# Sliding-window attention of a two-block network: how the softmax is shared between VectorE and ScalarE, and where a weight split stands

## The reference

```python
def one_block(args):
    qi, ki, vi, i = args
    s = jnp.einsum('bqkgd,bskd->bkgqs', qi, ki) + bias
    valid = in_band & ((i > 0) | key_in_own_block)
    s = jnp.where(valid, s, NEG_INF)
    m = jnp.maximum(s.max(-1, keepdims=True), sk)
    p = jnp.exp(s - m)
    p = p / (p.sum(-1, keepdims=True) + jnp.exp(sk - m))
    return jnp.einsum('bkgqs,bskd->bqkgd', p, vi)
```

## Time and profile before

| | |
|---|---|
| runs of the kernel before | 2300.67 us median of 3 (2295.68 to 2301.12) |
| profiled execution, its own time | 2301.37 us |
| its span in the profile | 2299.6 us |
| TensorE busy | 2152.4 us (94% of the span) |
| VectorE busy | 1436.4 us (62%) |
| ScalarE busy | 1020.3 us (44%) |
| GpSimd busy | 132.0 us (6%) |
| moved by transfers | 342.68 MB, 149 GB/s |

### The profile page before, as it was taken

How to read it: one execution, slowest core, us unless ns; L and a number is a source line. 1 busy time by engine, 2 the same in 40 slices (tenths; PEclk the granted TensorE clock), 3 DMA queues, 4 the chain that set the end, 5 groups by cost and what they waited for, 6 DMA issues and landing times.

```text
span 2299.6 us, 37741 instructions
## 1 busy us (share of the span) xinstructions
PE 2152.4 (94%) x16794; PEld 1955.7 (85%) x16794; DVE 1436.4 (62%) x1586; ACT 1020.3 (44%) x1051; POOL 132.0 (6%) x77
## 2 busy tenths in 40 slices
PE   6799999879999999899989999999998988899998
PEld 5778988769998997897778799899888966888996
DVE  8956655566655554866765665465468487657554
ACT  6564543544543443454553344344334437234442
POOL 1000000000001000400010020020022000102000
PEclk9899999999999999999999999999999999899999
DMA  7144555415555655563310466556555532124753
GB/s 192 17 154 146 183 191 174 147 37 165 184 175 179 205 182 175 165 203 113 125 56 2 147 211 192 177 174 201 180 163 186 165 117 103 39 73 148 216 179 119
DMA packets 259274, 342.68 MB, mean 149 GB/s; under 512 B 23111, under 2 KB 169197, under 8 KB 259111
## 3 DMA queue, kind: packets, MB, share of 16 engines
q1 hardware_dynamic: 253968, 329.95, 44.9%
q0 software_dynamic: 2544, 9.08, 1.3%
q10 hardware_dynamic: 2599, 1.23, 0.4%
HBM read 338.14 MB, written 2.10 MB: 148 GB/s over the span
## 4 chain that ended last, share of the span: by engine, by line
PE 78%; DVE 11%; ACT 6%; issue 2%; DMA 2%; POOL 0%; ACTq 0%; DVEq 0%; POOLq 0%
PE acc L1712 20%; PE acc L1713 20%; PE acc L1714 20%; DVE w_lo L1080 4%; PE acc L1728 3%; PE acc L2176 2%; ACT w_hi L638 2%; DMA raw<-in_w_in 1%; PE acc L2171 1%; PE acc L1735 1%; PE trp L1712 1%; PE acc L1777 1%; PE trp L2176 1%; PE trp L1713 1%; PE trp L1714 1%
## 5 line engine op out<-in xcount | busy, mean ns | idle before, releaser
L1080 DVE TENSOR_TENSOR w_lo<-raw,w_hi 128x2048 fp32r<-128x2048 f32 (+1 forms) x316 | 737.0, 2334 | 510.4 <-ACT w_hi L638 509.3
L638 ACT ACTIVATE w_hi<-raw 128x2048 fp32r<-128x2048 f32 (+1 forms) x316 | 593.5, 1879 | 643.7 <-PE acc L1714 283.0
L1712 PE MATMUL acc<-xT_hi,w_hi 128*128 128x256 f32 x2496 | 710.0, 284 | 16.7 <-DVE w_lo L1080 16.5
L1713 PE MATMUL acc<-xT_lo,w_hi 128*128 128x256 f32 x2496 | 709.3, 284 | 0.0
L1714 PE MATMUL acc<-xT_hi,w_lo 128*128 128x256 f32 x2496 | 709.0, 284 | 0.0
L1712 PEld LDWEIGHTS acc<-xT_hi,w_hi 128*128 128x128 f32 x2496 | 482.3, 193 | 18.0 <-issue 16.4
L1713 PEld LDWEIGHTS acc<-xT_lo,w_hi 128*128 128x128 f32 x2496 | 482.2, 193 | 0.0
L1714 PEld LDWEIGHTS acc<-xT_hi,w_lo 128*128 128x128 f32 x2496 | 482.2, 193 | 0.0
L1713 PE MATMUL acc<-w_lo,hT_hi 128*128 128x512 f32 x528 | 208.6, 395 | 0.0
L1714 PE MATMUL acc<-w_hi,hT_lo 128*128 128x512 f32 x528 | 208.6, 395 | 0.0
L1712 PE MATMUL acc<-w_hi,hT_hi 128*128 128x512 f32 x528 | 208.6, 395 | 0.0
(11 more groups left out here) (370 smaller groups left out, 2745.5 us busy)
## 6 DMA issues: line engine op xcount, KB each, us to landing
raw<-in_ffn_w SPq DMA_DIRECT2D x184, 512.0 KB
raw<-in_w_in SPq DMA_DIRECT2D x60, 1024.0 KB
raw<-in_ffn_w_up SPq DMA_DIRECT2D x88, 512.0 KB
raw<-in_ffn_w SPq DMA_DIRECT2D x40, 1024.0 KB
raw<-in_ffn_w_down SPq DMA_DIRECT2D x20, 1024.0 KB
raw<-in_ssm_w_glu SPq DMA_DIRECT2D x16, 512.0 KB
raw<-in_kv_w SPq DMA_DIRECT2D x8, 1024.0 KB
raw<-in_w_branch_a SPq DMA_DIRECT2D x8, 1024.0 KB
```

The costliest lines, as they stand in the source:

```text
L638: A(w_hi[:, p % SPL, 0:kt, :], raw[:, p % RAW, 0:kt, :], ACT.Copy).then_inc(hi_ready, 1)
L1080: V_.tensor_tensor(w_lo[:, p % SPL, 0:kt, :], raw[:, p % RAW, 0:kt, :], w_hi[:, p % SPL, 0:kt, :].bitcast(F32), ALU.subtract).then_inc(lo_ ...
L1712: mm(out, ah, bh, start=first, stop=False, skip_group_check=True)
L1713: mm(out, ah, bl, start=False, stop=False, skip_group_check=True)
```

## The change

The subtraction of the maximum leaves VectorE. Instead `r[1]` holds the negated maximum (`nsnk` is the negated sink, made once per layer), and ScalarE takes it as the bias of the exponential. A bias is one number per partition, and the tile has four rows of 128 per partition, so the one exponential becomes four. Each of them also gives the sum of its row (`accum_out`), and VectorE's row sum goes. `s_exp` now counts five for a step instead of two. `red` becomes two deep. On VectorE the split of the weights, which stood behind the masks at the end of a step, stands between the scores and the division.

```diff
                 def weights_exp(n):
                     act.wait_ge(sem("s_shifted"), 8 * i + n + 1)
-                    A(zA[:, n % 2], zA[:, n % 2], ACT.Exp).then_inc(sem("s_exp"), 1)
-                    A(red[:, 2, :], red[:, 2, :], ACT.Exp).then_inc(sem("s_exp"), 1)
+                    r = red[:, n % 2]
+                    for h in range(2):
+                        for b in range(2):
+                            q = slice(2 * h + b, 2 * h + b + 1)
+                            A(zA[:, n % 2, h, b, :], zA[:, n % 2, h, b, :], ACT.Exp, bias=r[:, 1, q], accum_out=r[:, 4, q]).then_inc(sem("s_exp"), 1)
+                    A(r[:, 2, :], r[:, 2, :], ACT.Exp).then_inc(sem("s_exp"), 1)
...
+                step(V_.tensor_scalar(nsnk[:, i], snk[:, i], -1.0, None, ALU.mult))
...
-                    do(V_.tensor_reduce(red[:, 0, :].rearrange("p (h b) -> p h b", h=2), z, AX_X, ALU.max))
-                    r = [red[:, q, :].rearrange("p (h b) -> p h b", h=2) for q in range(4)]
-                    sink = bc(snk[:, i, hs], 2, 2)
-                    do(V_.tensor_tensor(r[1], r[0], sink, ALU.max))
-                    do(V_.tensor_tensor(r[2], sink, r[1], ALU.subtract))
-                    V_.tensor_tensor(z, z, bc(r[1], 3, P), ALU.subtract).then_inc(sem("s_shifted"), 1)
+                    r = [red[:, n % 2, q, :].rearrange("p (h b) -> p h b", h=2) for q in range(5)]
+                    do(V_.tensor_reduce(r[0], z, AX_X, ALU.max))
+                    do(V_.scalar_tensor_tensor(r[1], r[0], -1.0, bc(nsnk[:, i, hs], 2, 2), ALU.mult, ALU.min))
+                    V_.tensor_tensor(r[2], bc(snk[:, i, hs], 2, 2), r[1], ALU.add).then_inc(sem("s_shifted"), 1)

                 def normalize(n):
...
-                    dve.wait_ge(sem("s_exp"), 2 * (8 * i + n + 1))
-                    do(V_.tensor_reduce(r[0], z, AX_X, ALU.add))
-                    do(V_.tensor_tensor(r[0], r[0], r[2], ALU.add))
-                    do(V_.reciprocal(r[3], r[0]))
+                    dve.wait_ge(sem("s_exp"), 5 * (8 * i + n + 1))
+                    do(V_.tensor_tensor(r[4], r[4], r[2], ALU.add))
+                    do(V_.reciprocal(r[3], r[4]))
                     V_.tensor_tensor(z, z, bc(r[3], 3, P), ALU.mult).then_inc(sem("s_normed"), 1)
...
-                split_lo(side_panel(i, 0)[2] + SPL)
                 for n in range(8 + 2):
                     if n < 8:
                         scores(n)
+                    split_lo(side_panel(i, n)[2] + SPL)
+                    if n < 8:
                         normalize(n)
                     if 1 <= n < 9:
                         mask_turned(n - 1)
-                    split_lo(side_panel(i, n + 1)[2] + SPL)
+                split_lo(side_panel(i, 10)[2] + SPL)
```

More of the change, by code:

```diff
@@ L200, in build @@
         snk = sb("snk", [P, DEPTH, HEADS])
+        nsnk = sb("nsnk", [P, DEPTH, HEADS])
         dng = sb("dng", [P, DEPTH, DK])
@@ L281, in build @@
         pT3 = sb("pT3", [P, 2, 3, P], F32, s4a)
-        red = sb("red", [P, 4, 4], F32, s4a)
+        red = sb("red", [P, 2, 5, 4], F32, s4a)
         s4a.close()
```

## The result

The changed kernel takes 2280.64 us (median of 4 runs, 2279.23 to 2287.62) against 2299.99 for the kernel before in the same comparison. The ratio is 0.9923, with a 95% interval of 0.9901 to 0.9944. A second measurement of the same kernel in another comparison gave 2278.44 us and 0.9904 (0.9884 to 0.9924). The prediction said 2279.5, range 2272 to 2287.

A forecast was written before the change was run, and what follows sets the result against it. VectorE was taken to set the loops' pace, 9.23 us a step against TensorE's 8.05. Waits of 14.9 us plus low clock of 6.2 made 21.2 us less: 2280.2 profiled, 2279.5 as median, range 2272 to 2287.

The forecast's parts named there:

- What bounds the loops: Second block's two loops: VectorE sets the pace, 9.23 us a step against TensorE's 8.05, which waits and loses clock.
- the gap: VectorE's row sum waits 0.79 us for the exponential in all eight steps; the moved split was to fill it.
- The sum: Both loops together: 14.9 us of TensorE's waits and 6.2 us of low clock saved, 21.2 us in all.
- group X: ScalarE's four exponentials with their row sums and L933 behind, each step: 2.15 us, ends 1.4 and 3.4.
- The weights: Later split frees its buffer later, but 8.4 us remain for a weight load of 5.4 us: hidden.
- The change part by part: VectorE's step in the loops: subtraction 0.69, row sum 0.72 and wait 0.79 go, leaving 7.03 us of work.
- The clock's 6.2 us: Four TensorE panels in the loops, 7.15 us at partly low clock, return to 5.59 each: 6.2 us gained.
- the first three: Loops: clock still falls, 2286, chance 0.10; ScalarE partly late, 2291, 0.07; accumulating pieces stop ScalarE, 2315, 0.03.
- turning point: Slower than before once ScalarE's group X reaches 4.35 us a step, that is 1.04 us a piece.
- The fourth: Behind the loops, the weights' transfers set the end, so the gain is given back: 2300 us, chance 0.05.
- the first one: Loops: waits go but TensorE still falls to 1.2 GHz, so only 14.9 us gained, 2286; chance 0.10.

The follow-up runs named there:

- The order alone: Against the kernel before, softmax unchanged and only the weight split moved between scores and division: 2279.62 us, ratio 0.9909.
- The softmax part alone: Against the changed kernel, the weight split put back at the end of the step, new softmax kept: 2300.05 us, ratio 0.9992.

## Why the prediction was right, step by step

- **What bounds the loops**: right. With the gap and the lead given to VectorE, TensorE's steps are 8.04 (8.05 stated), its waits 0.4 us twice (0.43 stated), the clock 1.00.
- **The sum**: 21.2 us stated, 21.7 measured in the loops, 19.4 and 23.8 by the medians of the two comparisons. The stated median, 2279.5, lies between the two measured ones; that it is within 1.2 us of both is in part luck, as these comparisons differ from each other by more.
- **ScalarE's group X**: 2.15 stated, 1.75 measured. The output of the sum was in no row, and I took 0.19 with nothing overlapping. It lasts 0.19 but overlaps like every other small activation, so it adds 0.09. The exponential with its pointer bias lasts 0.39 (0.40 stated), next start after 0.30.
- **The rule of the Trainium skill** on small tiles (page "VectorE: DVE Perf Modes", the section on the trn2 errata): the trace agrees on the fixed cost. The group of exponentials grew from 0.72 to 1.75 us a step, and ScalarE's busy time from 1020.3 to 1038.7 us. Only about 0.3 of the 1.0 us is the smaller tiles' by an estimate from the prediction's own rows (four plain pieces at 0.20 and L938 at 0.19, against 0.72). The bias adds some 0.4 and the sums 0.36. None of it cost time here, because the split covers it.
- **The weights**: right. No wait for a load appears in either loop.
- **The credit of the parts**: this is what I had wrong, though the total hides it. The change part by part reads as if VectorE's 1.41 us of removed work were needed to get under 8.05. The order alone brings 21.0 of 21.7 us. The softmax part alone brings 2.0, of which 1.6 are one panel's clock and 0.4 are pace. Behind the order it adds 0.7 us in the loops, less than the runs can tell. I compared steady periods and left out that a loop of eight steps can live on a small lead, here 0.8 us at its second pair of panels.
- **The clock's 6.2 us**: right as bookkeeping of TensorE's time, since waits and slow panels add up to what VectorE's pace cost. It isn't a second gain beside the waits: only the last panel of the first loop, 1.6 us, has no wait behind it that would take the time up.
- **Rivals**: the first three are excluded for this kernel (clock 1.00; X = 1.75; turning point measured beyond). The fourth is too, since the loops' 21.7 us reappear in the times, 19.4 and 23.8 us less by the medians. The ground on which I held the first one unlikely is weaker than I put it: one wait of 2.27 us in the kernel before has clock 1.00 behind it, from 1059 to 1065 us, so a long wait and a low clock don't always go together.

## What to carry to other kernels

In a short loop two periods aren't enough: ask also how far ahead the slower engine is, and how long that lasts. Here a lead of 0.8 us at the second pair of panels covered 0.3 us a step almost to the last pair. Look at two steps and not one when work recurs every second step; the softmax alone seemed to give 0.4 us a step and gave 0.08. Before work is taken off an engine, put independent work into its wait; here that alone brought nearly all, and the later savings only made idle time. A low clock in a stretch that waits for another engine is no loss of its own, as far as a wait follows that can take it up.

## What the runs showed of the hardware

An activation that gives its row sum shows as two instructions: ACTIVATE of 128x128 with a bias from memory, 385 to 405 ns, and ACTIVATION_READ_ACCUMULATOR, 185 to 190 ns. The pair starts again every 0.39 us. A filler product of 512 columns from the fp32 identity is two instructions and took 1.12 us. With one such filler in the wait the granted clock of the next panel was 1.00 in six of six places, three of which had read 0.79 without it. Without fillers the clock fell behind waits of 2.27, 2.34, 2.35 and 3.19 us, and didn't behind others of 2.27 and 2.36 us.
